# Moving filler matmuls inside an RWKV-7 recurrence: behind the block transposes, and into other groups of the last two slots

## The chip, the cores and the metric

The kernel runs on one core of one Trainium2 chip. The metric is the device time of one execution in microseconds, taken as the median of several runs. The kernel before takes 2473.57 us (three runs, 2472.69 to 2474.89).

The core's engines work side by side, each through its own list of instructions: PE multiplies matrices, DVE and ACT work on vectors and copy results out of PSUM, POOL does a few element-wise products and issues DMAs, SP issues the weight loads. They wait for each other through semaphores.

## The reference

The model has two layers over 256 tokens of width 2048. The first mixes time by RWKV-7, the second by block-sparse attention; each is followed by a layer norm, a SwiGLU network of width 5632 and another layer norm. The change touches only the recurrence of the first. Cut to that:

```python
def step(state, inp):                      # one state of 64x64 for each of 32 heads
    r_t, w_t, k_t, v_t, a_t, b_t = inp
    sa = einsum('bhij,bhj->bhi', state, a_t)
    state = (state * w_t[:, :, None, :] + sa[..., None] * b_t[:, :, None, :]
             + v_t[..., None] * k_t[:, :, None, :])
    return state, einsum('bhij,bhj->bhi', state, r_t)

v = xv @ w_v                               # 2048 x 2048
g = sigmoid(xg @ g1) @ g2                  # the gate
y = scan(step, 0, (r, decay, k, v, -kk, kk * a))
out = ((group_norm(y) + bonus) * g) @ w_o
```

## The kernel before, in words

All matrices are in float32. The large projections are split into a high and a low part and multiplied three times; they run before and after the recurrence and the change leaves them alone.

The recurrence does not walk through the tokens. It cuts them into chunks of 64 and solves, inside a chunk, a triangular system by five doubling steps. The 32 heads are taken in eight groups of four, one group a **slot** (`slot(s)`, L946, s from 0 to 7). Two lanes `a`, two heads each, stand beside each other. In step `l` of a slot PE runs `inner(s, l)` (L797, 16 matmuls of 64x64); DVE multiplies the result by a mask (L1876); PE runs `outer(s, l)` (L807); DVE transposes one copy of its result (L1882, L1884) while ACT keeps the other and moves it across partitions (L1396, L1381, L1382), and the next step can begin. The fifth step ends with L1402 and L1403.

Between these steps PE does other work of the same slot. For the group before (`s - 1`) it does `solutions` (L816), `chunks_of` for either lane (L828 to L858) and `state` 1 to 3 (L858 to L884). For the group after (`s + 1`) it does `decays` (L729, L732); behind `inner` 4 `transposes_of` (L746 to L750, whole 128x128 blocks), which ACT copies out in `turned` (L1373, L1377), once for each lane; `products` of the first lane (L762) ahead of `inner` 5 and of the second lane behind it; and at the end `values` (L781). DVE takes each lane's products in through `masked_products` (L1856, two predicated copies), and forms the next slot's first block from them. On DVE `masked_products` of the first lane stands ahead of the multiply of the fifth step.

Last there are **units**, single matmuls of 128x256 that belong to work which only has to be done by some later time: the value projection of head groups 4 to 7 (L914, 32 units a group) and the gate (L904, 4 units a group). `fill(n)` (L892) issues the next `n` of them. The table `FILL` (L59) says how many stand at each named place of each slot: `between("inner5")`, for instance, issues `FILL[s]["inner5"]` units behind `inner(s, 5)`. All places together hold 140 units and 20 stand ahead of slot 0. When a group of units ends, ACT copies it out (`keep`, L1405, or `keep_gate`, L1435), and the first unit of the next group waits for that copy. In slot 7, which has no group after it, transposes of finished outputs (`z_turned`, L929) stand where `transposes_of` and `products` stood.

The order on every engine is written out by hand; for ACT it is the loop at L1452, for DVE that at L1944. SP loads the weights for the units into a ring of four buffers; each load waits for the units that read the buffer before.

Of the kernel before, what the change touches and what calls it, by code (L numbers as in the profile page):

```python
# [54 lines left out]
LATE = GROUPS - EARLY  # L55
TURNS = [("value", 4), ("value", 5), ("gate", 0), ("gate", 1), ("value", 6), ("value", 7)] + [("gate", g) for g in range(2, GROUPS)]
UNITS = {"value": KT * TT, "gate": 2 * TT}
SOME = {"state1": 2, "inner3": 1, "outer3": 2, "outer4": 2, "inner5": 3, "outer5": 4}
FILL = (  # L59
    {"inner1": 3, "outer1": 2, "inner2": 2, "state1": 3, "inner3": 2, "outer3": 3, "outer4": 2, "inner5": 3, "outer5": 4},  # L60
    SOME,
    {"state1": 1, "inner3": 1, "outer3": 2, "outer4": 2, "inner5": 4, "outer5": 4},
    SOME,
    SOME,
# [3 lines left out]
)  # L68
WHOLE = 4
ZOUT = [(0, ch) for ch in range(WHOLE, 7)] + [(1, ch) for ch in range(7)] + [(0, 7), (1, 7)]  # L70
# [86 lines left out]
def trunk(nc, x, rows, rwkv_rows, lora, w, consts, ln_rows, y):  # L157
    with ExitStack() as ctx:
# [1097 lines left out]
        def _(act):  # L1256
# [58 lines left out]
            def decays(g):  # L1315

                act.wait_ge(cum_made, g + 1)
                act.wait_ge(nk_done, NJ)
                if g:
                    act.wait_ge(nat_done, g)  # L1320
                ci = ps[:, 4].rearrange("p (t c) -> p t c", t=TT)
                A(PC[:, g % 3].rearrange("p l c -> p (l c)"), ps[:, 6, 0:8], ACT.Exp)
                A(E[:, 0], ci, ACT.Exp)
                A(E[:, 1], ci, ACT.Exp, scale=-1.0).then_inc(cum_read, 1)

            def own_decays(g):

                cs = slice(g * 2 * P, (g + 1) * 2 * P)
                A(L_[:, :, cs], L_[:, :, cs], ACT.Exp, scale=DECAY).then_inc(decay_done, 1)
# [39 lines left out]
            def turned(g, a):  # L1369

                q = lq[a]
                act.wait_ge(q["tr_made"], g + 1)
                nc.scalar.copy(RI[g % 2][:, a, :, 0:2].rearrange("p j n c -> p n j c"),  # L1373
                               ps[:, 4 + 2 * a].rearrange("p (n j c) -> p n j c", n=2, j=4)).then_inc(q["arT_set"], 1)
                if g:
                    act.wait_ge(q["g_made"], g)
                nc.scalar.copy(BK[:, a], ps[:, 5 + 2 * a].rearrange("p (n t c) -> p n t c", n=2, t=TT)).then_inc(q["bkT_set"], 1)  # L1377

            def move(dst, src):

                nc.scalar.copy(dst[half(1)], src[half(0)])  # L1381
                return nc.scalar.copy(dst[half(0)], src[half(1)])  # L1382

            def value_part(g, a):

                q = lq[a]
                act.wait_ge(q["av_made"], g + 1)
                dst = L_[:, :, (2 * g + a) * P:(2 * g + a + 1) * P].rearrange("p t (h c) -> p h t c", h=2)
                src = ps[:, 5 + 2 * a, 0:2 * P].rearrange("p (h t c) -> p h t c", h=2, t=TT)
                (nc.scalar.copy(dst, src) if a else move(dst, src)).then_inc(q["av_set"], 1)  # L1390

            def outer(g, l, aside=None):

                act.wait_ge(ixt_made, 5 * g + l)
                if l < 5:
                    nc.scalar.copy(XT[g % 2][:, 0], ps[:, 0, T:2 * T]).then_inc(xt_kept, 1)  # L1396
                    if aside:
                        aside()
                    act.wait_ge(ix_turned, 4 * g + l)
                    move(XS, ps[:, 2, 0:T]).then_inc(ixt_set, 1)  # L1400
                else:
                    nc.scalar.copy(XT[g % 2][:, 0], ps[:, 0, T:2 * T])  # L1402
                    nc.scalar.copy(XT[g % 2][:, 1], ps[:, 2, 0:T]).then_inc(ixt_set, 1)  # L1403

            def keep(g):  # L1405

                act.wait_ge(fill_used, (g - EARLY + 1) * (KT // FK))
                nc.scalar.copy(V_[:, :, g * 2 * P:(g + 1) * 2 * P], ps[:, 3, :].rearrange("p (t c) -> p t c", t=TT)).then_inc(fill_copied, 1)

            def first(g):  # L1410

                act.wait_ge(first_set, g + 1)
                move(XS, XT[g % 2][:, 1]).then_inc(moved, 1)

            def squares(g):

                act.wait_ge(y_centred, g + 1)
                A(y_sq, R_[:, :, g * 2 * P:(g + 1) * 2 * P], ACT.Square).then_inc(y_squared, 1)

            def solutions(g, a):  # L1420

                q = lq[a]
                act.wait_ge(q["uhw_made"], g + 1)
                src = ps[:, 5 + 2 * a].rearrange("p (j n c) -> p j n c", j=4, n=2)
                (nc.scalar.copy(UHW[:, a], src) if a else move(UHW[:, a], src)).then_inc(q["uhw_set"], 1)

            def outputs(g):

                for a in (1, 0):
                    q = lq[a]  # L1430
                    act.wait_ge(q["y_made"], g + 1)
                    nc.scalar.copy(R_[:, :, (2 * g + a) * P:(2 * g + a + 1) * P].rearrange("p t (h i) -> p h t i", h=2),
                                   ps[:, 4 + 2 * a:6 + 2 * a, 0:P].rearrange("p h (t i) -> p h t i", t=TT)).then_inc(q["y_set"], 1)

            def keep_gate(g):  # L1435

                act.wait_ge(gate_made, g + 1)
                nc.scalar.copy(L_[:, :, g * 2 * P:(g + 1) * 2 * P], ps[:, 3, :].rearrange("p (t c) -> p t c", t=TT)).then_inc(gate_kept, 1)

            def keep_zt(g, bank):  # L1440

                act.wait_ge(z_tr, g + 1)
                nc.scalar.copy(zf[:, KC * g:KC * (g + 1)], ps[:, bank, :].rearrange("p (k t) -> p k t", k=KC)).then_inc(zt_kept, 1)
# [8 lines left out]
            for s in range(GROUPS):  # L1452
                more = s + 1 < GROUPS
                if s:
                    solutions(s - 1, 1)
                if s == 7:
                    outer(s, 1, lambda: (keep_gate(3), solutions(s - 1, 0)))
                else:
                    outer(s, 1, (lambda: solutions(s - 1, 0)) if s else None)
                if s and more:  # L1460
                    own_decays(s + 1)
                if s == 7:
                    keep_gate(4)
                outer(s, 2)
                if s == 7:
                    keep_gate(5)
                if s in (0, 5):
                    keep({0: 4, 5: 6}[s])
                outer(s, 3)
                if s:  # L1470
                    outputs(s - 1)
                if s == 7:
                    keep_gate(6)
                if more:
                    turned(s + 1, 0)
                outer(s, 4)
                if s == 7:
                    for g, bank in ((0, 4), (1, 6), (2, 5)):
                        keep_zt(g, bank)
                if s in (2, 6):  # L1480
                    keep({2: 5, 6: 7}[s])
                if more:
                    turned(s + 1, 1)
                if s == 2:
                    keep_gate(0)
                outer(s, 5)
                if more:
                    first(s + 1)
                if s in (2, 6):
                    keep_gate({2: 1, 6: 2}[s])  # L1490
                if more:
                    for a in (1, 0):
                        value_part(s + 1, a)
                if s:
                    squares(s - 1)
                if s + 2 < GROUPS:
                    decays(s + 2)
# [782 lines left out]
```

## Time and profile before

| | before |
|---|---|
| median of 3 runs | 2473.57 us |
| profiled execution | 2473.13 us, span 2471.3 us |
| PE busy | 2442.3 us (99%) |
| DVE busy | 1407.0 us (57%) |
| ACT busy | 1073.0 us (43%) |
| POOL busy | 129.6 us (5%) |
| granted PE clock | nine tenths or more of full speed in all 40 slices |

Four views of the profile are used. The page gives shares of the whole span. The chain of waits is followed back from the last instruction; it names, piece by piece, the work that the end stood on, or "issue", where an engine waited for nothing that the profile shows. The timeline gives the start and length of each instruction on one engine, with the idle time ahead of it and what ended that in brackets. A float32 matmul appears as two matmul records, so `x4` of L914 is two units. A single matmul's length overlaps with that of the next; what a group costs is the distance from its start to the next group's start, which is what the chain shows.

### The profile page before, as it was taken

What the parts mean: (1) busy time and instruction counts of PE and PEld (TensorE: products, weight loads), DVE (VectorE), ACT (ScalarE), POOL (GpSimd) and SP (SyncE); (2) the same over time, 40 slices, a digit from 0 to 9 for tenths busy, and PEclk for the clock granted to TensorE, in tenths of its full rate; (3) what the DMA queues carried; (4) which work ended last, traced back from release to release, by engine and by line L of the source; (5) the groups of instructions that cost most, each with busy time, mean ns of one, the idle gap of its engine ahead of it and who ended that gap; (6) DMA issues with size and microseconds to landing.
All of it is one profiled execution on the core that took longest, in us unless ns stands there. A gap on an engine that the chain in (4) does not pass through costs nothing.

```text
span 2471.3 us, 39453 instructions
## 1 busy us (share of the span) xinstructions
PE 2442.3 (99%) x15550; PEld 2003.7 (81%) x15550; DVE 1407.0 (57%) x1743; ACT 1073.0 (43%) x1348; POOL 129.6 (5%) x172
## 2 busy tenths in 40 slices
PE   8999999999999999999999999999999999999997
PEld 6888788877888888888887888888788888888886
DVE  7788566676744454454446644666745445444445
ACT  4455355444444444443334444453544444444332
POOL 2000235420000000000000000000000000000000
PEclk9999999999999999999999999999999999999999
DMA  6556411255666666666656665455566666666554
GB/s 235 188 192 209 128 42 40 69 210 190 193 192 188 187 193 188 187 187 195 192 193 204 198 195 188 147 176 179 180 187 193 188 187 190 187 201 212 194 194 140
DMA packets 225884, 440.88 MB, mean 178 GB/s; under 512 B 13616, under 2 KB 24240, under 8 KB 224672
## 3 DMA queue, kind: packets, MB, share of 16 engines
q1 hardware_dynamic: 221760, 417.38, 54.4%
q0 software_dynamic: 3600, 21.55, 2.6%
q8 instruction: 92, 1.51, 0.3%
q10 hardware_dynamic: 400, 0.18, 0.0%
q14 instruction: 32, 0.26, 0.0%
HBM read 436.96 MB, written 2.10 MB: 178 GB/s over the span
## 4 chain that ended last, share of the span: by engine, by line
PE 97%; DVE 1%; ACT 1%; DMA 1%; issue 0%; POOL 0%; DVEq 0%; SPq 0%; POOLq 0%
PE ps L601 26%; PE ps L603 26%; PE ps L602 26%; PE ps L914 3%; PE ps L1099 1%; PE ps L797 1%; PE ps L1127 1%; PE ps L807 1%; PE ps L630 1%; PE ps L628 1%; PE ps L629 1%; PE ps L858 1%; PE ps L904 1%; PE ps L762 1%; PE ps L941 1%; PE ps L1213 1%
## 5 line engine op out<-in xcount | busy, mean ns | idle before, releaser
L1270 ACT CAST whi<-raw 128x1024 fp32r<-128x1024 f32 x735 | 772.8, 1052 | 1143.7 <-PE ps L603 1087.2
L1713 DVE TENSOR_TENSOR wlo<-raw,whi 128x1024 fp32r<-128x1024 f32 x549 | 669.8, 1224 | 613.1 <-ACT whi L1270 611.1
L601 PE MATMUL ps<-whi,ahi 128*128 128x512 f32 x2172 | 852.0, 392 | 0.0
L603 PE MATMUL ps<-whi,alo 128*128 128x512 f32 x2172 | 846.3, 390 | 0.0
L602 PE MATMUL ps<-wlo,ahi 128*128 128x512 f32 x2172 | 845.7, 389 | 0.0
L603 PEld LDWEIGHTS ps<-whi,alo 128*128 128x128 f32 x2172 | 407.9, 188 | 85.3
L602 PEld LDWEIGHTS ps<-wlo,ahi 128*128 128x128 f32 x2172 | 408.1, 188 | 84.3 <-issue 1.0
L601 PEld LDWEIGHTS ps<-whi,ahi 128*128 128x128 f32 x2172 | 408.0, 188 | 83.6 <-DVE alo L2100 0.7
L2045 DVE TENSOR_TENSOR wlo<-raw,whi 128x1024 fp32r<-128x1024 f32 x193 | 236.1, 1224 | 249.8 <-ACT whi L1270 247.8
L601 PE MATMUL ps<-whi,hThi 128*128 128x512 f32 x656 | 255.6, 390 | 0.0
L603 PE MATMUL ps<-whi,hTlo 128*128 128x512 f32 x656 | 255.4, 389 | 0.0
L602 PE MATMUL ps<-wlo,hThi 128*128 128x512 f32 x656 | 255.4, 389 | 0.0
L603 PEld LDWEIGHTS ps<-whi,hTlo 128*128 128x128 f32 x656 | 123.2, 188 | 25.7
L601 PEld LDWEIGHTS ps<-whi,hThi 128*128 128x128 f32 x656 | 123.2, 188 | 25.5
L602 PEld LDWEIGHTS ps<-wlo,hThi 128*128 128x128 f32 x656 | 123.2, 188 | 25.3
L914 PE MATMUL ps<-raw,big 128*128 128x256 f32 x256 | 68.0, 398 | 0.4 <-issue 0.3
L577 POOL DMA_DIRECT2D big<-ln_rows x3 | 1.6, 536 | 1109.7 <-PE ps L630 786.7
L914 PEld LDWEIGHTS ps<-raw,big 128*128 128x128 f32 x256 | 44.7, 189 | 8.3 <-issue 1.1
L1544 ACT ACTIVATE a2t<-ps,lnT 128x128 f32<-128x128 f32 x96 | 34.1, 495 | 33.2 <-PE ps L1089 33.2
L1876 DVE TENSOR_TENSOR rec<-ps,big 128x512 f32<-128x512 f32 x40 | 27.5, 688 | 30.4 <-PE ps L797 30.4
L1721 DVE SCALAR_TENSOR_TENSOR big<-big,mixT 128x256 f32<-128x256 f32 x96 | 40.7, 479 | 0.5
L2147 DVE TENSOR_TENSOR hTlo<-ps,hThi 128x1024 f32 (+1 forms) x22 | 26.9, 1225 | 19.5 <-ACT hThi L1573 19.5
(317 smaller groups left out, 1941.8 us busy)
## 6 DMA issues: line engine op xcount, KB each, us to landing
raw<-w_up SPq DMA_DIRECT2D x176, 512.0 KB, 3.6
raw<-w_down SPq DMA_DIRECT2D x176, 512.0 KB, 4.0
raw<-w_gate SPq DMA_DIRECT2D x170, 512.0 KB, 3.6
raw<-w_k SPq DMA_DIRECT2D x32, 512.0 KB, 3.8
raw<-w_r SPq DMA_DIRECT2D x32, 512.0 KB, 4.4
raw<-w_v SPq DMA_DIRECT2D x32, 512.0 KB, 3.9
raw<-w_o SPq DMA_DIRECT2D x32, 512.0 KB, 5.1
raw<-kv_v SPq DMA_DIRECT2D x32, 512.0 KB, 3.7
```

The costliest lines, as they stand in the source:

```text
L601: mm(o, hi[:, k, tok], whi[:, s, k2, :], start=(k == 0), stop=False)
L602: mm(o, hi[:, k, tok], wlo[:, s, k2, :], start=False, stop=False)
L603: last = mm(o, lo[:, k, tok], whi[:, s, k2, :], start=False, stop=(k == kt - 1))
L628: mm(ps[:, 2 + t, :], hi[:, k, tok], wh[:, k2, :], start=False, stop=False)
L914: last = mm(ps[:, 3, t * T:(t + 1) * T], xxT[:, k, t * P:(t + 1) * P], rawf[:, s, k % FK], start=(i == 0), stop=(k == KT - 1), skip_group_ ...
L1270: nc.scalar.copy(whi[:, s], src).then_inc(hi_done, 1)
L1544: ins = A(hF[:, k, t * P:(t + 1) * P], ps[:, 4 + b, k2 * P:(k2 + 1) * P], ACT.Identity, scale=lnT[:, (n * 2) * KT + k:(n * 2) * KT + k + 1 ...
L1713: V.tensor_tensor(wlo[:, s], src, whi[:, s].bitcast(F32), ALU.subtract).then_inc(split_done, 1)
L1721: return V.scalar_tensor_tensor(out=out, in0=xxT[:, k], scalar=mixT[:, m * KT + k:m * KT + k + 1], in1=xT[:, k, 1:T + 1], op0=ALU.mult, op ...
L1876: V.tensor_tensor(Z.rearrange("p l (j c) -> p l j c", c=CHUNK), ps[:, 0:2, 0:4 * CHUNK].rearrange("p l (j c) -> p l j c", c=CHUNK), mask_l ...
L2045: V.tensor_tensor(wl, raw[:, s], wh.bitcast(F32), ALU.subtract).then_inc(split_done, 1)
L2147: V.tensor_tensor(hTlo[:, f0, :], ps[:, 4:6, :].rearrange("p a (k t) -> p (a k) t", k=2), hThi[:, f0, :].bitcast(F32), ALU.subtract).then_ ...
```

## The change

It moves entries of `FILL` and, on ACT, what has to move with them. The number of units in each slot stays the same, and so do their order and all other work of PE, DVE and POOL.

- In slots 0, 1, 3, 4 and 5 the three units behind `inner` 5 stand behind `transposes_of` (`inner4`). Slot 2 is unchanged.
- In slot 6 the two units at each of `inner1`, `outer1` and `inner2` stand behind `transposes_of`, six in all.
- In slot 7 the two units at `outer1` and the two at `inner2` go; `outer4` and `inner5` have four units each, not two.
- On ACT, where `inner4` has units and there is a next group, `turned` of the second lane stands ahead of the copies of `outer` 4, no longer behind them.
- In slot 7 the copies of gates 4, 5 and 6 (`keep_gate`) stand one or two steps later, behind the places where their units now end.

```diff
--- before.py
+++ after.py
@@ -55,16 +55,16 @@
 LATE = GROUPS - EARLY
 TURNS = [("value", 4), ("value", 5), ("gate", 0), ("gate", 1), ("value", 6), ("value", 7)] + [("gate", g) for g in range(2, GROUPS)]
 UNITS = {"value": KT * TT, "gate": 2 * TT}
-SOME = {"state1": 2, "inner3": 1, "outer3": 2, "outer4": 2, "inner5": 3, "outer5": 4}
+SOME = {"state1": 2, "inner3": 1, "outer3": 2, "inner4": 3, "outer4": 2, "outer5": 4}
 FILL = (
-    {"inner1": 3, "outer1": 2, "inner2": 2, "state1": 3, "inner3": 2, "outer3": 3, "outer4": 2, "inner5": 3, "outer5": 4},
+    {"inner1": 3, "outer1": 2, "inner2": 2, "state1": 3, "inner3": 2, "outer3": 3, "inner4": 3, "outer4": 2, "outer5": 4},
     SOME,
     {"state1": 1, "inner3": 1, "outer3": 2, "outer4": 2, "inner5": 4, "outer5": 4},
     SOME,
     SOME,
-    {"state1": 2, "inner3": 2, "outer3": 3, "outer4": 2, "inner5": 3, "outer5": 4},
-    {"inner1": 2, "outer1": 2, "inner2": 2, "state1": 4, "inner3": 2, "outer3": 4, "outer4": 4, "outer5": 4},
-    {"inner1": 4, "outer1": 2, "inner2": 2, "state1": 2, "inner3": 2, "outer3": 2, "inner4": 2, "outer4": 2, "inner5": 2},
+    {"state1": 2, "inner3": 2, "outer3": 3, "inner4": 3, "outer4": 2, "outer5": 4},
+    {"state1": 4, "inner3": 2, "outer3": 4, "inner4": 6, "outer4": 4, "outer5": 4},
+    {"inner1": 4, "state1": 2, "inner3": 2, "outer3": 2, "inner4": 2, "outer4": 4, "inner5": 4},
 )
 WHOLE = 4
 ZOUT = [(0, ch) for ch in range(WHOLE, 7)] + [(1, ch) for ch in range(7)] + [(0, 7), (1, 7)]
@@ -1459,27 +1459,28 @@
                     outer(s, 1, (lambda: solutions(s - 1, 0)) if s else None)
                 if s and more:
                     own_decays(s + 1)
+                outer(s, 2)
                 if s == 7:
                     keep_gate(4)
-                outer(s, 2)
-                if s == 7:
-                    keep_gate(5)
                 if s in (0, 5):
                     keep({0: 4, 5: 6}[s])
                 outer(s, 3)
                 if s:
                     outputs(s - 1)
                 if s == 7:
-                    keep_gate(6)
+                    keep_gate(5)
+                beside = FILL[s].get("inner4", 0) > 0
                 if more:
-                    turned(s + 1, 0)
+                    for a in range(2 if beside else 1):
+                        turned(s + 1, a)
                 outer(s, 4)
                 if s == 7:
+                    keep_gate(6)
                     for g, bank in ((0, 4), (1, 6), (2, 5)):
                         keep_zt(g, bank)
                 if s in (2, 6):
                     keep({2: 5, 6: 7}[s])
-                if more:
+                if more and not beside:
                     turned(s + 1, 1)
                 if s == 2:
                     keep_gate(0)
```

PE in slot 4, from the transposes of the next group to the fifth `outer` (a row is one group of matmuls of a line, with its shape; `x3` of L914 are three units):

```order
 L747 MATMUL ps<-ident,big 128x2x64
 L750 MATMUL ps<-ident,big 128x128 x4
+L914 MATMUL ps<-raw,big 128x256 x3
 L807 MATMUL ps<-rec 64x64 x16
 L914 MATMUL ps<-raw,big 128x256 x2
 L762 MATMUL ps<-a2t,rec 64x128 x16
 L797 MATMUL ps<-rec 64x64 x16
-L914 MATMUL ps<-raw,big 128x256 x3
 L762 MATMUL ps<-a2t,rec 64x128 x16
 L807 MATMUL ps<-rec 64x64 x16
```

The three units move from between `inner` 5 (L797) and the second `products` (L762) to a place between the transposes and `outer` 4 (L807).

ACT in slot 4, from the first lane's `turned` to the end of the fifth step (with the semaphores waited for):

```order
 L1373 COPY a2t<-ps 128x2x4x64 [waits lane0_tr_made]
 L1377 COPY rec<-ps 128x512 [waits lane0_g_made]
-L1396 COPY rec<-ps 128x256 [waits ixt_made]
-L1381 COPY rec<-ps 64x256 [waits ix_turned]
-L1382 COPY rec<-ps 64x256
 L1373 COPY a2t<-ps 128x2x4x64 [waits lane1_tr_made]
 L1377 COPY rec<-ps 128x512 [waits lane1_g_made]
+L1396 COPY rec<-ps 128x256 [waits ixt_made]
+L1381 COPY rec<-ps 64x256 [waits ix_turned]
+L1382 COPY rec<-ps 64x256
 L1402 COPY rec<-ps 128x256 [waits ixt_made]
 L1403 COPY rec<-ps 128x256
```

The second lane's two copies pass the three copies of `outer` 4.

PE in slot 6, behind the decays; two more pairs of units, behind either `chunks_of`, go in the same way:

```order
 L732 MATMUL ps<-big 128x2 x4
 L816 MATMUL ps<-big,a2t 64x128 x16
-L914 MATMUL ps<-raw,big 128x256 x2
 L807 MATMUL ps<-rec 64x64 x16
 L828 MATMUL ps<-a2t 64x64 x2
```

`outer` 1 now follows `solutions` (L816) directly.

## Rows read from the trace of the kernel before

**Rows 1.** The page: busy time, share of the span, instructions; and the chain that ended last

```profile
PE 2442.3 (99%) x15550; PEld 2003.7 (81%) x15550; DVE 1407.0 (57%) x1743; ACT 1073.0 (43%) x1348; POOL 129.6 (5%) x172
...
PE 97%; DVE 1%; ACT 1%; DMA 1%; issue 0%; POOL 0%; DVEq 0%; SPq 0%; POOLq 0%
```

**Rows 2.** Chain, slot 4, fifth step: start us, us, engine, tile, line, records

```profile
410.10 1.06 PE ps L914 x4
411.16 1.03 PE ps L762 x32
412.19 0.46 PE ps L797 x32
412.66 1.49 PE ps L914 x6
414.15 1.03 PE ps L762 x32
415.19 0.46 PE ps L807 x32
415.65 1.93 PE ps L914 x8
417.57 0.62 PE ps L781 x32
418.20 0.47 PE ps L797 x32
```

**Rows 3.** Chain, units behind the first transposes

```profile
277.97 2.59 PE ps L914 x12
```

**Rows 4.** Timeline of DVE, slot 4: start, us, operation, [idle before, releaser]

```profile
412.33 1.35 DVE L1856 COPY_PREDICATED a2t<-big,ps 128x512 f32<-128x512 uint32 x2 [0.26 <-PE ps L762]
```

**Rows 5.** Chain, slot 6, fifth step

```profile
468.56 1.08 PE ps L762 x32
...
469.74 1.35 DVE a2t L1856 x2
...
471.80 0.69 PE ps L807 x32
...
475.04 0.47 PE ps L797 x32
```

**Rows 6.** Timeline of ACT, slot 4, second lane's copy

```profile
411.97 0.59 ACT L1377 COPY rec<-ps 128x512 f32<-128x512 f32 x1
```

**Rows 7.** Chain, slot 4, first steps

```profile
392.34 0.47 PE ps L797 x32
...
399.03 0.81 issue
...
401.45 1.06 PE ps L914 x4
```

**Rows 8.** Chain, slot 6, first steps

```profile
444.57 0.47 PE ps L797 x32
...
455.84 0.41 PE ps L914
```

**Rows 9.** Timeline of PE, slots 1, 3 and 5: three of five gaps

```profile
322.50 0.21 PE L858 MATMUL ps<-big,rec 64*64 64x64 f32 x1 [0.63 <-issue]
...
375.26 0.33 PE L884 MATMUL ps<-a2t 64*64 64x64 f32 x4 [1.24 <-issue]
...
427.33 0.70 PE L914 MATMUL ps<-raw,big 128*128 128x256 f32 x2 [0.34 <-issue]
```

**Rows 10.** The page, DMA queues: packets, MB, share

```profile
q8 instruction: 92, 1.51, 0.3%
```

**Rows 11.** Timeline of ACT, slot 7, first lane's solutions

```profile
480.60 0.58 ACT L1382 COPY a2t<-ps 64x512 f32<-64x512 f32 x1
```

**Rows 12.** Chain, slot 7, first units of the state step

```profile
485.60 1.06 PE ps L904 x4
```

**Rows 13.** Timeline of POOL, slot 7, start of finish(4)

```profile
489.25 0.19 POOL L466 TENSOR_TENSOR idle<-idle 128x1 f32<-128x1 f32 x1
```

## The prediction

> **What bounds the kernel now.** I read the shares of the page first: the PE is busy for nearly the whole span, and the chain that ended last is PE for 97% [rows 1]. So a change pays only where it alters PE work or PE waits. The stretch touched is the recurrence, 276 to 499 us: eight slots of some 26 us, numbered 0 to 7. Then I read the chain of waits slot by slot. In slot 4 the fifth step has no wait: from the start of the first `products` (L762, 411.16) to the first inner product of the next slot (L797, 418.20) are 7.04 us, each piece starting where the one before ended [rows 2]. Slots 0, 1, 3 and 5 read the same, to 0.01 us. The fill units (L914 or L904) are small pieces of independent projection work, there to cover waits.
>
> Two prices come from these rows. Two records are one unit: groups of 2, 3 and 4 units take 1.06, 1.49 and 1.93 us [rows 2], so a unit costs 0.43 us and a group 0.20 us more. The following 64-row group starts 0.15 us late as well: L762 takes 1.03 us behind a fill, while two 16-matmul groups of 64x64 take 0.62 us (L781) behind a fill and 0.46 us (L797) behind other 64-row work [rows 2]. Beside 128-row transposes the surcharge is absent: 12 records behind them take 2.59 us, 0.43 us a unit [rows 3].
>
> The rule that bears on the surcharge is in the Trainium skill, "TensorEngine Tiling (Array Packing)", section Key Properties: changing the tiling mode, not just the tile, drains TensorE. The trace agrees in kind, with 0.35 us for a pair of changes. By that rule alone, fewer changes make a faster kernel; this is the first rival below.
>
> **Part 1: slots 0, 1, 3, 4 and 5, three units from the fifth inner step to behind the transposes.** Added at the new place: 3 x 0.43 = 1.29 us on the path. Nothing hides them, because the transposes alone already last longer than the multiply on DVE that `outer` 4 waits for; the PE does not wait there now. Removed at the old place: 1.49 us, and 0.14 us of `products` behind it, 1.63 us in all.
>
> But these three units cover a wait. DVE takes the products in with two predicated copies, 1.35 us, and only then multiplies for the fifth step; it starts at 412.33, 1.17 us after the first `products` began [rows 4]. Without the units the PE is through `products`, `inner` 5 and `products` 2.4 us after that start, and must wait for DVE. Slot 6 shows this already, since it has no unit there: `products` starts at 468.56, DVE's copies at 469.74 (1.18 us later, as in slot 4), `outer` 5 only at 471.80, 3.24 us after the start, and the next slot's L797 at 475.04 [rows 5]. That is 6.48 us for what takes 7.04 us in slot 4, with the same four units behind `outer` 5. So of the 1.63 us removed only 0.56 us are won; the rest is a wait for DVE and a restart behind it. A slot: 1.29 - 0.56 = +0.73 us; five of them: **+3.65 us**. Bounds: -0.34 us a slot if no wait appeared (1.29 - 1.63), +1.29 us if the removal won nothing. I take slot 6, the same sequence on all engines.
>
> The copies of the second lane (L1373, L1377) move ahead of the fourth step's copies on ACT. Now they end at 412.56 [rows 6]; `products` of that lane would want them at T0 + 1.5 us, T0 being its first `products`, which then is just met. Ahead of `outer` 4 they need about 1.3 us from the end of the transposes, and `outer` 4 then ends 1.29 + 0.62 = 1.9 us behind that end. What is queued behind them on ACT, the copy of `outer` 4 for which `inner` 5 and `outer` 5 wait, is therefore not late: 0, with 0.3 us a slot at most if it were.
>
> **Part 2: slot 6.** Six units leave three groups of two (behind `solutions` and both `chunks_of`) and go behind the transposes. There they cost 6 x 0.43 = 2.58 us. What the removal wins is read from slot 4, which has no units in those places. From the first L797 to the first unit of `state1`: slot 4, 392.34 to 401.45, 9.11 us; slot 6, 444.57 to 455.84, 11.27 us [rows 7, 8]. Won 2.16 us, not the 3 x 1.21 = 3.6 us of PE work, because slot 4 has waits there: on ACT, and 0.81 us in which nothing in the profile is waited for [rows 7]. Net **+0.42 us**; bounds -1.05 (all 3.6 won) and +0.9 (slot 3, whose same stretch is 9.61 us because its gap is 1.24 us).
>
> That gap of the kind "issue" stands once in each of slots 1 to 5, 0.34 to 1.24 us, and in none of slots 0, 6 and 7 [rows 9]. It stands in the densest run of small matmuls, inside a group, so no operand explains it. Code reaches the engines in packets of 1.51 MB / 92 = 16 KB [rows 10]. Counting instructions between the gaps (a float32 matmul leaves two loads and two matmuls), I find them at multiples of one block size, five or six blocks apart, and each gap ends 3.3 to 3.9 us after the block boundary before it. I read it as code that is late when a block runs faster than about 3.5 us. The Trainium skill, "Advanced Engine Details and Errata", section ISA Cache, says that a line of 16 KB holds 256 instructions and that there are only 2 lines; the spacing agrees, and by it taking fills out of such a run brings a gap back.
>
> **Part 3: slot 7.** Four units leave the groups behind both `chunks_of` and go to `outer4` and `inner5`, whose groups exist already beside 128-row transposes: 4 x 0.43 = +1.72 us, nothing there waits. Won at the old place: PE work of 2 x (1.06 + 0.15) = 2.42 us. Then the second `chunks_of` waits for ACT's copy, which ends at 481.18 [rows 11], where the PE would be there at 480.98: 0.25 us with the hand-over. And by the block count a boundary stands at about 480.45 and the next inside `state` 1; the gap would end 3.5 us later, at 483.95, and `state1`'s units start at 484.4 instead of 485.60 [rows 12]. Won 1.2 us, net **+0.5 us**; bounds -0.5 (no gap) and +0.8 (gap of 1.24 us). The gate copies on ACT shift by one or two steps with their units; each still has 1.07 us (transposes and one `inner` or `outer`) before the next gate starts, for a copy of 0.6 us. POOL's `finish(4)` wants gate 4 at 489.25 [rows 13] and, by the shifts above, has it just before. Cost 0.
>
> **The sum.** 3.65 + 0.42 + 0.5 = +4.6 us. The path leaves the recurrence on PE, and the weight loads for the output projection are released by PE's own fills, so all later work shifts by the same amount. The profiled execution took 2473.13 us (span 2471.3), so 2477.7; the median of the runs is 0.44 us above it: **2478.1 us**, +0.19%.
>
> **Rivals.**
> Mode changes decide (faster): the waits I add are hidden, and each group taken from between 64-row groups wins its 0.35 us: 5 x 0.34, 3 x 0.35 and 2 x 0.35, together -3.5 us, 2470.1 us. For it: the surcharge is in every row. Against it: slot 6 shows the wait for DVE in exactly the new order. It decides if DVE's copies began right at `products`' first half. Chance 0.12, a third of which may pass -0.2%.
> No code gap comes back in slots 6 and 7: slot 6 ends at -0.4, slot 7 at -0.5, in all +2.8 us, 2476.4 us. For it: these slots have none now. Against: slots 1 to 5 have one. Chance 0.12.
> Code is late in the fifth step too (slower): `products`, `inner`, `products` and `outer` stand in a row there now, and if two block boundaries fell less than 3.5 us apart, a slot would lose another 0.8 us beyond the wait for DVE: +4.0 us, 2482.1 us. It decides only where a boundary is in the first `products` and the next before `outer` 5; my count sees at least 4.5 us between them, and slot 6 has no such gap. Chance 0.12.
>
> **How the numbers follow.** Forecast 0.64; its own range is 2476.8 to 2479.6, from the spread of the gaps (+-0.5 us a slot in two slots) and +-0.15 us a slot in five. A measurement of this kernel can tell about 0.2%, 4.95 us, from no change: the line is 2478.5 us. Of the forecast's 0.64 some 0.25 lie above it and 0.39 below. Slower: 0.25 + 0.12 = 0.37. Within: 0.39 + 0.12 + 0.07 = 0.58. Faster: 0.05. The range 2474.8 to 2481.0 holds the forecast and the second rival, part of the third, and leaves out the first.
>
> **What would show it.** In slots 0, 1, 3, 4 and 5 the first `products` to the next slot's L797 should take 6.5 us, with about 0.4 us of L807 waiting for DVE L1876, and the group behind the transposes should take 1.29 us, not 1.49. Slot 6 should have an issue gap of about 0.8 us between `chunks_of` and `state`, slot 7 one inside `state` 1. Each of the five slots should be 0.7 us longer. It is wrong if the wait for L1876 stays under 0.2 us, or if the slots get shorter.

## The result, and the profile after

The kernel after takes 2476.82 us (median of 22 runs, 2475.67 to 2478.69) against 2473.34 for the kernel before (22 runs, 2470.94 to 2475.72). The ratio is 1.0015, 95% interval 1.0009 to 1.0021, so +3.5 us (2.2 to 5.2). The forecast was 2478.1 us, range 2474.8 to 2481.0. The change makes the kernel slower by a little less than I said. The profiled execution took a span of 2474.8 us, 3.5 us more than before.

The page after, the rows that answer to [rows 1]. PE is busy for 1.4 us less. Its share of the chain fell from 97% to 95%, but that is not the change: in this execution the chain passes through a weight load (`raw<-w_k`, 15.31 us from 25.29 on), long before the recurrence, and the kernel with `outer` 4's units moved below, which is as fast as before, has the same shares. What changed must be read in the recurrence itself:

```profile
PE 2440.9 (99%) x15550; PEld 2002.9 (81%) x15550; DVE 1408.2 (57%) x1743; ACT 1072.5 (43%) x1348; POOL 129.8 (5%) x172
...
PE 95%; DMA 2%; DVE 1%; ACT 1%; issue 0%; POOL 0%; SPq 0%; DVEq 0%
```

The chain after, slot 4, from the units behind the transposes to the next slot (start us, us, what), beside [rows 2]:

```profile
411.06 1.30 PE ps L914 x6
412.35 0.62 PE ps L807 x32
412.98 1.06 PE ps L914 x4
414.04 1.08 PE ps L762 x32
...
415.21 1.35 DVE a2t L1857 x2
416.56 0.58 DVE rec L1877
...
417.28 0.69 PE ps L807 x32
417.97 1.92 PE ps L914 x8
419.90 0.62 PE ps L781 x32
420.52 0.47 PE ps L797 x32
```

The group behind the transposes costs 1.30 us. Then the chain leaves PE: it goes from the first `products` (L762) through DVE's two predicated copies and its multiply (L1857 and L1877, which were L1856 and L1876) to `outer` 5. From the first `products` to the next slot's L797 are 6.48 us, where 7.04 stood. PE's own row for that `outer` 5 shows the wait (idle before and releaser in brackets):

```profile
417.28 0.69 PE L807 MATMUL ps<-rec 64*64 64x64 f32 x32 [0.87 <-DVE rec L1877]
```

Where the time went, slot by slot. A slot runs from its first L797 to the next slot's; slot 7 ends at the first output projection (L941). The numbers in parentheses are gaps of the kind "issue" inside it. One more of 0.22 or 0.23 us stands at the end of slot 7, ahead of `solutions` (L816), in every kernel of this document; it is left out of the table and of all sums of gaps.

| slot | before | after | part 1 alone | slot 6 alone | slot 7 alone |
|---|---|---|---|---|---|
| 0 | 22.66 | 23.34 | 23.33 | | |
| 1 | 25.74 (0.63) | 26.52 (0.74) | 25.99 (0.19) | (0.63) | (0.90) |
| 2 | 26.29 (1.08) | 25.74 (0.53) | 25.99 (0.91) | (0.65) | (0.81) |
| 3 | 26.36 (1.24) | 26.02 (0.17) | 26.09 (0.23) | (0.44) | (0.44) |
| 4 | 25.86 (0.81) | 26.68 (0.88) | 26.42 (0.61) | (0.79) | (0.53) |
| 5 | 26.37 (0.34) | 26.51 | 26.50 | (0.20) | |
| 6 | 30.47 | 30.64 (0.48) | 30.47 | 30.70 (0.54) | |
| 7 | 25.51 | 26.08 (0.09) | 25.51 | | 26.08 (0.03) |

Without their gaps slots 0 and 1 grew by 0.68 and 0.67 us, slots 3 and 4 by 0.73 and 0.75, and the unchanged slot 2 by nothing. Slot 5 grew by only 0.48 in this way, but its gap of before stands ahead of units and cost more than the 0.34 us that PE's records show as idle: from `state1`'s units to the first `products` took 11.17 us before and 10.57 in the three kernels below that have waits put in, where no gap falls into it. After, it takes 11.87, which is 10.57 and the 1.30 us of the group. The rest of the slot, from the first `products` to the next L797, went from 6.93 to 6.37 us. (These are starts in the timeline; between them this stretch is 0.1 us shorter than in the chain.) So slot 5 counts as +0.73 too. Five slots: 3.56 us. Slot 6 adds 0.17, slot 7 0.57, in all 4.3 us. The slots as they stand differ by only 2.3 us, since the gaps of slots 1 to 5 sum to 4.10 us in this one execution before and to 2.32 in the one after; the recurrence also began 0.94 us later, ahead of any changed instruction, and the start varies from one execution to the next, from 275.2 to 277.7 us in the profiles here (the one with waits put directly ahead of it left out). So the two profiles agree with the medians by an accident of these terms; the slot times without the gaps are what the change did.

The new gap of slot 6, a row of the timeline of PE after. Slot 6 had none before:

```profile
454.26 0.27 PE L858 MATMUL ps<-a2t 64*64 64x64 f32 x2 [0.48 <-issue]
```

Slot 7 after: timeline of PE, then the chain. `chunks_of` of the second lane waits for ACT, the gap inside `state` 1 is only 0.09 us (pieces of 0.01 to 0.14 us of "issue" stand in the chain where it changes engines, too), `state1`'s units start at 486.70, and later a gate's first unit waits for ACT's copy of the gate before (L1438):

```profile
483.87 0.36 PE L828 MATMUL ps<-rec,a2t 64*64 64x64 f32 x8 [0.26 <-ACT a2t L1382]
...
498.67 1.99 PE L904 MATMUL ps<-rec,big 128*128 128x256 f32 x8 [0.30 <-ACT big L1438]
```

```profile
485.94 0.09 issue
486.03 0.50 PE ps L858 x9
...
486.70 1.06 PE ps L904 x4
...
495.08 1.28 DVE gsm L1698
...
496.78 0.46 DVE rec L1883
497.26 0.36 ACT rec L1381
497.63 0.37 ACT rec L1382
498.03 0.59 ACT big L1438
```

### The profile page after: what moved, and what is told of

It reads as the page before. It is cut to its first block, busy times and chain, and to the rows that moved or that the text cites. A ratio compares the mean times of both kernels' runs of the same rounds, so it can differ in the third digit from the quotient of the medians.

```text
span 2474.8 us, 39453 instructions
## 1 busy us (share of the span) xinstructions
PE 2440.9 (99%) x15550; PEld 2002.9 (81%) x15550; DVE 1408.2 (57%) x1743; ACT 1072.5 (43%) x1348; POOL 129.8 (5%) x172
## 4 chain that ended last, share of the span: by engine, by line
PE 95%; DMA 2%; DVE 1%; ACT 1%; issue 0%; POOL 0%; SPq 0%; DVEq 0%
PE ps L601 26%; PE ps L603 26%; PE ps L602 26%; PE ps L914 3%; PE ps L1099 1%; PE ps L807 1%; PE ps L1127 1%; PE ps L630 1%; PE ps L628 1%; PE ps L629 1%; PE ps L797 1%; PE ps L858 1%; DMA raw<-w_k 1%; PE ps L941 1%; PE ps L1213 1%; PE ps L1211 1%
## 5 line engine op out<-in xcount | busy, mean ns | idle before, releaser
L914 PE MATMUL ps<-raw,big 128*128 128x256 f32 x256 | 66.6, 395 | 0.1
L914 PEld LDWEIGHTS ps<-raw,big 128*128 128x128 f32 x256 | 45.0, 189 | 7.1 <-ACT big L1408 0.2
L1877 DVE TENSOR_TENSOR rec<-ps,big 128x512 f32<-128x512 f32 x40 | 27.5, 687 | 28.4 <-PE ps L797 28.4
```

The lines of the kernel that those rows point to most:

```text
L914: last = mm(ps[:, 3, t * T:(t + 1) * T], xxT[:, k, t * P:(t + 1) * P], rawf[:, s, k % FK], start=(i == 0), stop=(k == KT - 1), skip_group_ ...
L1877: V.tensor_tensor(Z.rearrange("p l (j c) -> p l j c", c=CHUNK), ps[:, 0:2, 0:4 * CHUNK].rearrange("p l (j c) -> p l j c", c=CHUNK), mask_l ...
```

## The experiments

Every kernel is set against the kernel before, on the same chip. Edits are cut to the lines that tell the change; of `FILL` only the row of slots 1, 3 and 4 is shown. The theory is the prediction's: units cost 0.43 us each wherever they stand bare, the three units covered a wait for DVE, and the gaps are code that comes late.

### The parts by themselves

Three kernels, each with one part of the change: slots 0, 1, 3, 4 and 5; slot 6; slot 7.

```diff
-SOME = {"state1": 2, "inner3": 1, "outer3": 2, "outer4": 2, "inner5": 3, "outer5": 4}
+SOME = {"state1": 2, "inner3": 1, "outer3": 2, "inner4": 3, "outer4": 2, "outer5": 4}
```

> Only the first part: in slots 0, 1, 3, 4 and 5 the three units stand behind the transposes, with the second lane's copies on ACT moved; slots 6 and 7 as before. Theory (units covered a wait for DVE): +0.73 us a slot, +3.65 us in all, with 0.38 us of L807 waiting for DVE L1876 in each of the five slots and 6.48 us from the first products to the next L797. Rival A (mode changes decide): -0.34 us a slot, -1.7 us in all, and no such wait. Rival B (code that comes late decides, and the wait in front of it gives it time): the gaps of kind issue in slots 1 to 5 shrink from 3.95 us together to about 2.2 us as in the profile after, so that the whole is only +1.9 us.

> Only slot 6 changed: six units from three groups to behind its transposes. Slots 1 to 5 are the code of before, so their gaps are a second sample of the old order: if the gaps are only chance from one execution to the next, they differ from 0.63, 0.93, 1.24, 0.81 and 0.34 us; if they belong to the order, they are the same within 0.1 us. Theory: +0.4 us, with one gap of 0.3 to 1.2 us between chunks_of and state in slot 6. Rival A (mode changes decide): -1.05 us. Rival B (no gap comes back): -0.4 us.

> Only slot 7 changed: four units from behind chunks_of to outer4 and inner5, with the gate copies on ACT. Theory: +0.5 us. Rival A (mode changes decide): -0.7 us. Rival C (in the changed tail PE waits for DVE and ACT, as the profile after shows at the fourth step, where two scalar operations of the group norm took 0.83 and 1.28 us): first part -1.5 us, tail +2.1 us, together +0.6 us, of which the 0.4 us above the price of four units is a wait in the tail.

Part 1 alone: 2476.70 us against 2473.20, ratio 1.0014 (1.0005 to 1.0023). Slot 6 alone: 2473.06, ratio 1.0002 (0.9993 to 1.0011). Slot 7 alone: 2473.17, ratio 1.0000 (0.9991 to 1.0009). So nearly all of the loss is part 1. Its slots read as in the kernel after; the wait in slot 4 (timeline of PE, part 1 alone):

```profile
417.55 0.69 PE L807 MATMUL ps<-rec 64*64 64x64 f32 x32 [0.88 <-DVE rec L1878]
```

The other two can't be told from no change by their totals, but their own slots changed by +0.23 and +0.57 us, as in the kernel after. Slot 6 alone has the gap at the same kind of matmul, slot 7 alone has the wait for ACT (timelines of PE):

```profile
450.79 0.27 PE L858 MATMUL ps<-a2t 64*64 64x64 f32 x2 [0.54 <-issue]
```

```profile
481.01 0.36 PE L828 MATMUL ps<-rec,a2t 64*64 64x64 f32 x8 [0.27 <-ACT a2t L1382]
...
495.80 0.92 PE L904 MATMUL ps<-rec,big 128*128 128x256 f32 x3 [0.35 <-ACT big L1438]
```

### ACT's order as before

Part 1 with the second lane's copies behind those of `outer` 4 again.

```diff
-                beside = FILL[s].get("inner4", 0) > 0
+                beside = False
```

> The first part again, but the second lane's copies on ACT stay behind the copies of outer 4. Theory: products of the second lane then wait for ACT, as in slot 6 before (0.25 us of L762 waiting for ACT L1377), but outer 5 waits for DVE anyway, so the time is that of the first part alone, within 0.3 us. Rival D (the new order on ACT is what the change needs): 0.25 us a slot more than the first part alone, +1.2 us beyond it.

2476.59 us, ratio 1.0014 (1.0005 to 1.0024), the same as part 1 with the move (2476.70). The recorded wait of `outer` 5 is 0.59 us instead of 0.88, since the second `products` starts 0.2 us later (1.62 us behind the first, not 1.39), but it ends at the same event, DVE's multiply, and the stretch is as long. The ACT move is worth nothing, as forecast.

### DVE's multiply ahead of its copies

The kernel after, with DVE's multiply of the fifth step ahead of the first lane's predicated copies.

```diff
-                if more:
-                    masked_products(s + 1, 0)
                 inner(s, 5)
                 if more:
+                    masked_products(s + 1, 0)
                     first_block(s + 1, 0)
```

> The changed kernel, but on DVE the multiply of the fifth step stands ahead of the predicated copies of the first lane's products, so that outer 5 finds its operand ready. Theory (DVE's own work from the products to the next slot's first block is the floor: two times two copies 2.5 us, the multiply 0.6, two first blocks 0.8, one transpose 0.6, behind 1.2 us of products, together 6.3 us): the wait of L807 goes from 0.8 us to under 0.1 us, but values or the next L797 wait instead, and the first products to the next L797 stays at 6.3 to 6.5 us; the time is that of the changed kernel within 0.5 us. Rival A (only the wait of outer 5 stands in the way): 0.8 us less in six slots, -4.8 us against the changed kernel, faster than before by 1.3 us.

2479.94 us (8 runs), ratio 1.0028 (1.0017 to 1.0038): 3.1 us slower than the kernel after, where I had expected no more than 0.5 either way. `outer` 5 no longer waits, but the next slot does (timeline of PE, slot 4):

```profile
421.79 0.69 PE L781 MATMUL ps<-big,a2t 64*64 64x64 f32 x32 [0.34 <-DVE a2t L1857]
423.00 0.69 PE L797 MATMUL ps<-rec,a2t 64*64 64x64 f32 x32 [0.51 <-DVE rec L1872]
```

The chain shows why: DVE is now the chain from `inner` 5 to the next slot's first block, and the copies that stood ahead of the multiply stand in the middle of it:

```profile
418.00 0.69 DVE rec L1877
418.69 1.26 DVE a2t L1857 x2
...
419.98 0.43 DVE a2t L1866
420.40 1.25 DVE a2t L1857 x2
...
421.68 0.44 DVE a2t L1866
...
422.14 0.72 DVE rec L1872
```

The rival, that the wait at `outer` 5 is a matter of DVE's order alone and could be had back for nothing, is refuted. Between `products` and the next slot the turned order takes 0.35 us a slot more than the order of before (6.65 to 6.73 us instead of 6.30 to 6.37). Expected was that DVE's work takes the same time in either order, and that was wrong. Without their gaps all slots together are 2.6 us longer than in the kernel after: 2.1 in six such stretches, 0.25 in slot 7. The remaining 0.5 us of the 3.1 were not traced.

### One unit left behind

Part 1, with two units behind the transposes and one still behind `inner` 5.

```diff
-SOME = {"state1": 2, "inner3": 1, "outer3": 2, "inner4": 3, "outer4": 2, "outer5": 4}
+SOME = {"state1": 2, "inner3": 1, "outer3": 2, "inner4": 2, "outer4": 2, "inner5": 1, "outer5": 4}
```

> The first part alone, with one of the three units left behind inner 5 and two behind the transposes. Theory: PE's work up to outer 5 is then 3.15 us, just under the 3.24 us at which DVE's result is there, so the unit is free: the first products to the next L797 stays 6.3 to 6.4 us as with none, and only 0.86 us are added behind the transposes, not 1.29. A slot +0.30 us against before, five +1.5 us (first part alone: +3.6). The wait of L807 falls from 0.8 to 0.1 us. Rival A (mode changes decide): one unit keeps both changes, a slot 0.35 us worse than with none.

2474.04 us, ratio 1.0007 (0.9998 to 1.0016). The stretch with the group behind the transposes grew by 0.87 us, two units, and the last one by nothing against part 1: 6.30 and 6.38 us, with 0.08 us of waiting (chain, slot 4):

```profile
415.03 0.63 PE ps L914 x2
415.66 1.03 PE ps L762 x32
416.69 0.08 issue
416.77 0.69 PE ps L807 x32
```

So one unit fits into the wait for nothing, and the loss is 0.24 to 0.32 us a slot instead of 0.67 to 0.75. (Slot 4 of this execution lost 0.53 without its gap; 0.2 of that lies ahead of the transposes, where nothing was changed.) This is the prediction's account of part 1 turned round: of the 1.63 us removed 1.07 were cover for DVE.

### Units from places that seemed to cover nothing

The kernel before, with the two units behind `outer` 4 moved behind the transposes in slots 0 to 5; and, on top of it, the unit behind `inner` 3 in slots 1 to 4.

```diff
-SOME = {"state1": 2, "inner3": 1, "outer3": 2, "outer4": 2, "inner5": 3, "outer5": 4}
+SOME = {"state1": 2, "inner3": 1, "outer3": 2, "inner4": 2, "inner5": 3, "outer5": 4}
```

> Before, but the two units behind outer 4 (not those behind inner 5) stand behind the transposes, in slots 0 to 5. Theory: PE work falls by 1.06 + 0.15 - 0.86 = 0.35 us a slot, and the three units behind inner 5 still cover DVE (its copies start 2.0 us after outer 4, PE reaches outer 5 at 3.9 us when the operand is just ready): -0.35 us a slot, -2.1 us in all, with at most 0.2 us of L807 waiting. Rival (DVE is late by what stands behind outer 4): DVE's group norm keeps the copies off until 2.0 us after outer 4, the fifth step loses what the group wins, 0 in all.

> As the run before, and the one unit behind inner 3 also goes behind the transposes in slots 1 to 4. Theory: its group costs 0.63 + 0.15 us and 0.43 us beside the transposes, so -0.35 us a slot if outer 3 finds its operand; PE has 0.6 us of state work between inner 3 and outer 3 and DVE needs 0.7 us, so 0.1 to 0.2 us come back as a wait of L807 for L1876: -0.2 us a slot in four, -0.8 us beyond the run before, -2.9 us against before. Rival: state work on DVE stands ahead of that multiply and makes the wait 0.4 us or more, so nothing is won.

2473.55 us, ratio 1.0003 (0.9994 to 1.0012), and 2474.84, ratio 1.0005 (0.9996 to 1.0014). In the first, the slots without their gaps are about as long as before (22.65 us in slot 0, 25.09 in slot 1, 0.07 more than before in slots 3 and 4) and not 0.35 us shorter. Slot 2 is 0.40 us longer, since the first unit of the next gate now waits 0.36 us for ACT's copy (L1408). One pair of mode changes went, and `inner` 5 now waits for DVE's transposes of `outer` 4 (chain, slot 4):

```profile
410.07 0.67 PE ps L807 x32
...
410.83 0.45 DVE rec L1882
411.28 0.34 DVE rec L1884
...
411.67 0.69 PE ps L797 x32
```

In the second, `outer` 3 waits for the multiply as well (timeline of PE), and slots 1, 3 and 4 are 0.33 to 0.36 us longer than in the first without their gaps, a loss where -0.2 us was expected:

```profile
406.23 0.69 PE L807 MATMUL ps<-rec 64*64 64x64 f32 x32 [0.46 <-DVE rec L1876]
```

So none of these removals won more than the units cost at their new place: behind `inner` 5 they won 0.56 to 0.63 us for 1.30, behind `outer` 4 0.8 to 0.9 for 0.87, behind `inner` 3 about 0.1 for 0.43. The rest was cover for a wait. The first rival of the prediction, mode changes decide, is refuted here as well: in each case the pair of changes went, and its 0.35 us did not come.

### What the gaps are

The kernel before, with 128 waits on a load that landed long ago ahead of the recurrence on PE.

```diff
+            for _ in range(128):
+                pe.wait_ge(id_in, 16)
             transposes_of(0)
```

> Before, with 128 waits (on a load that landed long ago) put into PE's instructions once, ahead of the first transposes (L746, 276 us); nothing else changed. In before the gaps of kind issue stand at a fixed matmul in each slot: in slot 1 inside the L858 matmuls of the second half of the first state step (322.50), in slot 3 at its L884, in slot 5 in the units behind it. Theory, late code: what is late is fixed by the instruction's place in the program. 128 instructions are 32 float32 matmuls, 64 records, so every gap moves 64 records toward the start: in slot 1 to the L837 matmuls of the second lane's chunks (2.3 us earlier), in slot 3 to L858 of the same (2.9 us earlier), in slot 5 to L858 as well (2.65 us earlier), and the slot times without the gaps stay within 0.1 us. Rival, an operand or a buffer that those matmuls wait for and that the profile doesn't name: the gaps stay at the same matmuls (L858, L884, the units) whatever stands ahead. Total: within 2 us of before in either case.

One run each: 2474.47 us against 2471.19, where I had expected them within 2 us of each other. The recurrence starts 2.6 us later, but 0.9 of that lies ahead of the waits, in the projection. PE's idle time ahead of its first transpose went from 1.15 to 2.78 us, so the waits cost 1.6 us:

```profile
278.61 0.30 PE L746 MATMUL ps<-ident,big 128*128 128x128 f32 x1 [2.78 <-issue]
```

The page counts 39517 instructions where before has 39453, so the 128 waits became 64 instructions, two waits in each. Timeline of PE, all gaps of the slots, but for the one of 0.22 us at L816 that every kernel has:

```profile
324.04 0.21 PE L807 MATMUL ps<-a2t,rec 64*64 64x64 f32 x1 [0.23 <-issue]
...
374.61 0.27 PE L807 MATMUL ps<-a2t,rec 64*64 64x64 f32 x2 [0.23 <-issue]
...
425.49 0.27 PE L807 MATMUL ps<-rec 64*64 64x64 f32 x1 [0.55 <-issue]
...
495.11 0.27 PE L807 MATMUL ps<-rec 64*64 64x64 f32 x1 [1.40 <-issue]
```

The gaps moved, though no operand of these matmuls changed; the rival, an unnamed operand, is refuted. In slot 1 the gap of before stood ahead of the twelfth record of an L858 group [rows 9]; ahead of that group stand the 32 records of `outer` 2, and the gap now stands ahead of the twelfth of those. 32 records and their 32 weight loads are 64 instructions, exactly what was put in. I had said 64 records, counting a wait as one instruction. The gaps of slots 2 and 4 are gone and slot 7 has one of 1.40 us.

Does the position pay? Two more kernels put the waits between the 128x512 matmuls of the projection ahead of the recurrence, where PE has time for them: 64 instructions, one between two matmuls, and 224, two between two. `beside` issues those waits until all are out.

```diff
                         mm(o, hi[:, k, tok], whi[:, s, k2, :], start=(k == 0), stop=False)
+                        beside()
                         mm(o, hi[:, k, tok], wlo[:, s, k2, :], start=False, stop=False)
+                        beside()
```

> Before with the shift of the last run (64 more instructions on PE ahead of the recurrence), but put one at a time between the 128x512 matmuls of the projection that runs ahead of it, 0.227 us each, where they should cost nothing. Late code theory: the first L746 stands at 276.0 again (not at 278.6), no gap in slots 2 and 4, gaps of slots 1, 3 and 5 inside `outer` 2 (L807) as in the run before, their sum near 1 us instead of before's 4.1; in slot 7 a gap inside an L807, as there. Total 1 to 3 us below before, 2470.3 to 2472.3. Rival, the gaps of the run before were small by luck (they vary from 0.17 to 1.39 us at one and the same place): positions as said, but the sum of all gaps 3 us or more and the total within 1 us of before.

> The same with 224 instructions instead of 64, two between two matmuls. Blocks of 256 instructions: a shift of 224 earlier is one of 32 later, so the gaps move 16 records toward the end from where they are in before: slot 1 from the middle of L858 (second half of the first state step) to its end or L884, slot 3 from L884 into the units L914 behind it, slot 2 from L837 to its end. If the block were not 256 instructions the gaps would stand anywhere else, for instance 112 records earlier. Sizes: a boundary among 128x256 units has more time to the one before, so smaller gaps: sum near 2.5 us, total 0 to 2 us below before (2471.3 to 2473.3). Rival, sizes by luck: total as before within 1 us.

With 64: 2474.35 us against 2473.29, ratio 1.0004 (0.9995 to 1.0013). The waits cost nothing now: PE's idle time ahead of the first transpose is 1.15 us as in before, and the matmuls of the projection still follow each other every 0.227 us. But the total is no lower, where I had expected 1 to 3 us less. And the gaps of slots 1, 3, 5 and 7 stand inside the same L807 groups as in the run before (L816 in this kernel's numbering), but with other sizes: 0.80, 0.52, 0.55 and 1.13 us, and small ones of 0.20 to 0.27 us in slots 2 and 4; in all 3.7 us. Its rival is right: the positions of the larger gaps are the program's, the sizes are not. With 224: 2472.11 us, ratio 0.9995 (0.9986 to 1.0004). Two gaps are left in this execution, in slots 2 and 4. Both stand 16 records, 32 instructions, later in the code than those of before, as a shift of 32 instructions in blocks of 256 asks; slots 1 and 3 have none, where I had expected them (L867 and L816 are `chunks_of`'s L858 and `outer` 2's L807). Timeline of PE:

```profile
346.77 0.27 PE L867 MATMUL ps<-a2t 64*64 64x64 f32 x1 [0.73 <-issue]
...
398.36 0.63 PE L816 MATMUL ps<-rec 64*64 64x64 f32 x27 [0.90 <-issue]
```

This is the lowest median of all kernels here, and its interval holds 1: it can't be told from before. No version was found that measurably beats the kernel before.

## Why the prediction was right

**Part 1, the group behind the transposes (+1.29 us a slot): right.** 1.30 us in slot 4, and the stretch from `state1`'s units to the first `products` went from 9.70 to 11.00 us in slots 1, 3 and 4.

**Part 1, what the removal wins (-0.56 us): right.** PE's records show -0.57 us in slots 3 to 5 and -0.63 in slots 0 and 1. Slot 6 of before was the right model for the stretch, though not, as the prediction says, the same sequence on all engines: there ACT's copy for the second lane stands behind those of `outer` 4. That is why the wait was put at 0.4 us and is 0.79 to 0.87. In slot 6 of before the second `products` first waits for that copy (timeline of PE):

```profile
470.31 1.10 PE L762 MATMUL ps<-a2t,rec 64*64 64x128 f32 x32 [0.25 <-ACT rec L1377]
471.80 0.69 PE L807 MATMUL ps<-rec 64*64 64x64 f32 x32 [0.38 <-DVE rec L1876]
```

The change moves the copy ahead; the second `products` then starts 1.39 us behind the first and not 1.82, and `outer` 5 waits that much longer, in slot 6 after too (0.86 us). The prediction's own times, PE through at 2.4 us and `outer` 5 at 3.24, ask for 0.8. It changed no sum, since DVE and not PE sets the end. With one unit back (0.08 us of waiting, no loss) and with DVE's order turned (a new wait) both sides of this step were tried. Five slots: 3.56 us measured, 3.65 forecast.

**Part 2, slot 6 (+0.42): right in its terms, smaller in size.** The gap came back at the place said, between `chunks_of` and `state`, with 0.48 and 0.54 us instead of 0.8, and the slot grew by 0.17 and 0.23 us. Without the gap it would have been 0.3 us shorter, as the second rival had it (-0.4).

**Part 3, slot 7 (+0.5): the sum right, two of its terms wrong.** The sum is +0.57, in both kernels that have the change. The wait for ACT is 0.26 us, as said. The gap inside `state` 1 is there, but PE's idle time in it is only 0.09 and 0.03 us. With the records around it, which take longer, it costs 0.35 to 0.4 us: from `state` 1's first L858 behind `outer` 2 to `state1`'s units are 1.08 and 1.03 us where before has 0.68. The sum used 1.0. Ahead of it 0.2 us less was won than forecast (the second `chunks_of` starts 0.78 us earlier in the slot, not 0.96). So the first part of the slot won 1.53 us (10.67 to 9.14) and not 1.2. Behind it the four units cost 2.10 us and not 1.72. Gates end later and in larger groups, and the first unit of the next gate waits 0.30 us for ACT's copy of the one before; ACT had been held by the copies of `outer` 4, and these by DVE, where one 128x8 operation of the group norm took 1.27 us (its like take 0.17). "Nothing there waits" was wrong, and so was the size of the gap; that the sum came out is luck, since the two errors cancelled.

**ACT's move and the gates (0): the move right**, by its own experiment; the gate copies cost the 0.30 us above.

**The rivals.** Mode changes decide: refuted, by the kernel after and by the two that moved other groups. Code late in the fifth step too: no changed kernel has a gap between the first `products` of a slot and its `outer` 5. No gap comes back: nearly right in slot 7, wrong in slot 6. On the gaps of before the prediction was not exact: slot 2 has two, of 0.93 and 0.15 us, and slot 7 has the one at L816. The two lines that it takes from the Trainium skill, "Advanced Engine Details and Errata", section ISA Cache, do not fit PE: the same list gives 128 KB for TensorE, which at 16 KB a line would be eight. No sum rests on that.

**The total.** The terms as measured give 3.56 + 0.2 + 0.57 = 4.3 us, the medians 3.5 (2.2 to 5.2). The difference of 0.8 us lies inside the interval; whether the gaps of slots 1 to 5 are on average shorter in the new program stays open. They sum to 4.10, 2.71 and 2.68 us in the three programs with the old code there (before, slot 6 alone, slot 7 alone), to 2.63 and 4.33 with units of `outer` 4 and `inner` 3 moved, and to 2.32, 1.94, 3.03, 3.71 and 3.91 in the five that moved units from behind `inner` 5, which tells no difference.

## What to carry to other kernels

A filler between two steps of a dependent chain is worth what it covers: before it is moved, find the releaser that stands next in line, here DVE's copies and multiply 1.2 us behind the first `products`, and count only what is left above it. A slot of the same kernel that already has the new order is the best estimate there is: slot 6 gave 0.56 us where the sum of removed work gave 1.63. Beside the wide transposes nothing waited here, and each unit put there cost its full 0.43 us.

## What the runs showed of the hardware

The gaps of kind "issue" in runs of 64x64 matmuls belong to the place of the code: 64 instructions put in far ahead moved one by exactly 64 instructions (32 records), and the gap stands at one and the same matmul in all programs with equal code ahead of it, up to the few instructions moved. The Trainium skill, "Advanced Engine Details and Errata", section ISA Cache, gives lines of 16 KB that hold 256 instructions; a shift of 224 earlier behaved as one of 32 later, which agrees. The size is not fixed by the program: the gap of slot 3 was 0.17 to 1.24 us in kernels that have it at the same L884, that of slot 1 0.19 to 1.39. What makes it vary was not found, and that the gaps are late loading of code is argued from their places alone; no row shows the loading.

128 waits on a semaphore that was already set delayed PE's next matmul by 1.6 us, 0.026 us for each of the 64 instructions that they became (one execution); between 128x512 matmuls they cost nothing.

On DVE, too, single small operations of the group norm last long. From the start of slot 7 on, three 128x8 operations stand out, whose like take 0.17 us. In all ten programs here with the slot 7 of before they are the same three, with 0.85, 1.26 and 1.28 us in the kernel before. In the three with the new slot 7 (after, slot 7 alone, DVE's multiply first) the third is another operation, 21 operations earlier, which takes 1.26 or 1.27 us (L1698, L1697 in the kernel before, where it takes 0.17). DVE's own order there was not changed, so its place in DVE's code alone does not decide. What does was not tested.
